# A hybrid retention and SSD layer on eight cores: convolution in one PSUM bank, the skip term on GpSimd, one matmul to spread four heads, and dependences kept by 8 bytes

## The reference

```python
h = x + hybrid_mixer(rmsnorm(x), w_in, ...)        # retention, 4 heads of 256; SSD, 16 heads of 64
y = rmsnorm(h + squared_relu_mlp(rmsnorm(h), w_up, w_down))
# in the mixer, for the SSD heads:
xbc = silu(causal_depthwise_conv(xbc, conv_w) + conv_b)     # 4 taps over time, 1536 channels
xs, bm, cm = split(xbc, [1024, 1280])
L = exp(where(causal, a_cs[l] - a_cs[s], -inf))             # per chunk of 128 tokens and head
y_diag = ((cm @ bm.T) * L) @ (xs * dt)
state  = exp(a_cs[-1]) * state + bm.T @ (xs * dt * exp(a_cs[-1] - a_cs))
y_ssd  = y_diag + exp(a_cs) * (cm @ state_before) + d_skip * xs
y_ssd  = rmsnorm_per_group(y_ssd * silu(z))
```

## Time and profile before

| | |
|---|---|
| median of 3 runs | 1701.88 us (1701.72 to 1702.16) |
| the profiled execution | 1701.95 us |
| its span, first to last instruction, slowest core (2) | 1700.4 us |
| spans of the eight cores | 1697.8 to 1700.4 us |
| mean granted TensorE clock, every core | 0.998 |
| PE busy | 1651.5 us, 97% |
| VectorE (DVE) busy | 704.2 us, 41% |
| ScalarE (ACT) busy | 404.0 us, 24% |
| GpSimd (POOL) busy, nearly all of it DMA issues | 66.3 us, 4% |

### The profile page before, as it was taken

The page is one execution under the profiler, slowest core; times in us unless marked ns, Lnnn a source line. Parts: engine busy times, 40 slices in busy tenths (PEclk is TensorE's granted clock), DMA queues, the critical chain, the costliest instruction groups (busy, mean ns, idle before and its releaser), DMA issues.

```text
span 1700.4 us, 26583 instructions; the slowest of 8 cores (1697.8 to 1700.4 us)
## 1 busy us (share of the span) xinstructions
PE 1651.5 (97%) x10277; PEld 962.3 (57%) x10410; DVE 704.2 (41%) x1300; ACT 404.0 (24%) x767; POOL 66.3 (4%) x127
## 2 busy tenths in 40 slices
PE   3999999999999999999999999999999999999997
PEld 2898888776666676545444444444444444444443
DVE  4577657777765555537312111212111211221235
ACT  4532325767622222102111001110001100011013
POOL 2000000000000000000000000000000000000000
PEclk9999999999999999999999999999999999999999
DMA  9965527333293264761854456443554443554425
GB/s 241 234 115 105 89 32 112 54 73 50 31 194 55 46 100 62 178 109 16 135 78 70 69 81 95 78 76 50 92 82 75 75 75 60 90 85 79 86 65 156
DMA packets 23099, 155.09 MB, mean 91 GB/s; under 512 B 2560, under 2 KB 2816, under 8 KB 5696
## 3 DMA queue, kind: packets, MB, share of 16 engines
q0 software_dynamic: 17648, 124.92, 45.1%
q1 hardware_dynamic: 5328, 28.48, 5.3%
HBM read 261.06 MB, written 8.39 MB: 158 GB/s over the span
## 4 chain that ended last, share of the span: by engine, by line
PE 94%; DMA 2%; DVE 1%; issue 1%; ACT 1%; DVEq 0%; POOL 0%; ACTq 0%; POOLq 0%
PE psum L513 92%; PE psum L516 2%; DMA arena<-xp 1%; DMA arena<-cstb 1%; DVE arena L541 1%; ACT arena L534 1%; DVE arena L550 0%; DVE arena L545 0%; ACT L534 0%; DVEq L372 0%; DVEq L391 0%; POOL arena L503 0%; ACTq L391 0%; POOLq L391 0%; POOLq L443 0%
## 5 line engine op out<-in xcount | busy, mean ns | idle before, releaser
L513 PE MATMUL psum<-arena 128*128 128x512 bf16 (+6 forms) x9541 | 1617.5, 329 | 13.8 <-DVE arena L541 4.9
L513 PEld LDWEIGHTS psum<-arena 128*128 128x128 bf16 x9674 | 917.0, 98 | 694.6 <-issue 12.8
L541 DVE TENSOR_TENSOR arena<-arena 128x512 bf16<-128x512 f32 (+6 forms) x351 | 191.1, 550 | 376.7 <-ACT arena L534 367.2
L534 ACT ACTIVATE arena<-psum 128x512 f32<-128x512 f32 (+4 forms) x234 | 130.9, 565 | 793.4 <-PE psum L513 759.2
L541 DVE TENSOR_TENSOR arena<-arena,psum 128x512 f32<-128x512 f32 x190 | 130.1, 687 | 367.7 <-PE psum L513 356.2
L534 ACT ACTIVATE arena<-arena 128x512 bf16<-128x512 f32 (+3 forms) x207 | 151.5, 744 | 377.2 <-DVE arena L541 174.5
L541 DVE TENSOR_TENSOR arena<-psum,arena 128x512 f32<-128x512 f32 (+5 forms) x250 | 175.6, 731 | 134.0 <-PE psum L513 111.8
L550 DVE SCALAR_TENSOR_TENSOR arena<-psum,arena 128x512 f32<-128x512 f32 (+1 forms) x164 | 112.0, 695 | 44.5 <-ACT arena L534 38.3
L534 ACT ACTIVATE arena<-psum,arena 128x128 f32<-128x128 f32 (+3 forms) x212 | 91.4, 514 | 108.8 <-PE psum L513 86.1
L516 PE MATMUL psum<-arena 128*128 128x128 bf16 x736 | 56.7, 225 | 24.9 <-DVE arena L545 24.7
L516 PEld LDWEIGHTS psum<-arena 128*128 128x128 bf16 x736 | 48.7, 101 | 32.8 <-issue 26.5
(11 more groups left out here) (18 smaller groups left out, 21.5 us busy)
## 6 DMA issues: line engine op xcount, KB each, us to landing
arena<-w_up POOLq DMA_DIRECT2D x32, 1024.0 KB, 10.9
arena<-w_down POOLq DMA_DIRECT2D x32, 1024.0 KB, 10.3
arena<-w_ret POOLq DMA_DIRECT2D x22, 1024.0 KB, 10.6
arena<-xm SPq DMA_DIRECT2D x16, 1024.0 KB, 10.4
arena<-w_xs POOLq DMA_DIRECT2D x8, 1024.0 KB, 10.9
arena<-w_out POOLq DMA_DIRECT2D x8, 1024.0 KB, 10.9
arena<-xp POOLq DMA_DIRECT2D x7, 1024.0 KB, 26.9
y<-arena SPq DMA_DIRECT2D x14, 512.0 KB, 3.6
```

The costliest lines, as they stand in the source:

```text
L513: P.op("pe", lambda e: e.matmul(R(out), lhsT=lhsT, rhs=rhs, start=start, stop=stop), [lhsT, rhs], [out], c, lat=163.0)
L534: P.op("act", lambda e: e.activation(out=R(out), in_=R(in_), func=func, **kw), ins, outs, c, lat=0.0, table=table)
L541: P.op(eng, lambda e: e.tensor_tensor(out=R(out), in0=R(a), in1=R(b), op=op), [a, b], [out], dcost(out, True), lat=0.0)
```

## The change

- `XW` is 1024: no halo in `xnP` and `xnM`. `convtile` makes 512 columns at once in one bank, 16 matmuls (the first-block tiles of group 0 in P in two halves of 256). The taps that fall ahead of the tile come from `tail`: the last three PSUM columns of the tile before are copied, five small POOL operations combine them with the taps, and a 3-column addition puts them into the next tile. `chead` makes the last four columns of P for the two channel tiles that P doesn't compute.
- The skip term is a product on POOL of the transposed x with d_skip, added to `t1` on POOL; `dgh`, `dgl` and their matmuls go. The product for the state input and the decay of the state also move from DVE to POOL.
- `spread` holds the running sums of each of four heads in its own 128 columns, zero on the other heads' partitions (made with the mask `hm`), and 16 more rows with a mask by blocks of 8 tokens. One matmul of 512 columns then takes the place of the mask matmul and the four of a head. Inside a block of 8 the values above the diagonal can become large; the product with the decay takes the minimum with 1e30 first, and the scores are masked by `tri` as before.
- `GR` is 8. The planner's model gets other DMA figures, POOL is no longer held to the order of the text, operations on PSUM tiles that aren't on PE get a priority of 1000 places, and costs of small matmuls and of POOL change.
- The selection matrix is smaller and is loaded ahead of `dtM`; the transfer of the old mask goes.

```diff
-XW = 1028
+XW = 1024
-GR = 32
+GR = 8
-DMA_SHARE = {"sp": 1.0, "pool": 1.4}
-DMA_START = {"sp": 1500.0, "pool": 4000.0}
+DMA_PULL = {"sp": 0.5, "pool": 1.0}
+DMA_START = {"sp": 1500.0, "pool": 6000.0}
+AHEAD = 1000
-    INORD = ("pool", "sp")
+    INORD = ("sp",)
...
+        rank = list(range(len(recs)))
+        for ops in self.vops:
+            for i in ops:
+                if recs[i]["eng"] != "pe":
+                    rank[i] = i - AHEAD
...
+    def dcost(out, two, eng="dve"):
         n = float(np.prod(out.shape[1:]))
+        if eng == "pool":
+            return 200.0 + 2.2 * n
         return 150.0 + (1.045 if two else 0.55) * n
...
-    def convtile(xn, w, co, ch, blk, out):
-        p2 = bank("C", 2).rearrange("p (s n) -> p s n", s=2)
-        for s in range(2):
-            t0 = (2 * blk + s) * 256
+    tails = {}
+
+    def tail(ch, h):
+        k = tails.get(ch, 0)
+        tails[ch] = k + 1
+        cp(raw[:, ch, k % 2, :], h)
+        h, g, t = raw[:, ch, k % 2, :], head[:, ch, :], htmp[:, ch, :]
+        ts(g, h, cw[:, 0, ch:ch + 1], None, ALU.mult, eng="pool")
+        for j in (1, 2):
+            ts(t[:, 0:3 - j], h[:, j:3], cw[:, j, ch:ch + 1], None, ALU.mult, eng="pool")
+            tt(g[:, 0:3 - j], g[:, 0:3 - j], t[:, 0:3 - j], ALU.add, "pool")
+
+    def convtile(xn, w, co, ch, blk, out, parts=1):
+        p = bank("C")
+        n = 512 // parts
+        for s in range(parts):
+            t0 = blk * 512 + s * n
             for dc in range(16):
-                mm(p2[:, s, 0:260], w[:, dc, co:co + 128], xn[:, dc, t0:t0 + 260], dc == 0, dc == 15)
-        acc = accr().rearrange("p (s n) -> p s n", s=2)
-        act(acc, p2[:, :, 4:260], AF.Identity, scale=cw[:, 3, ch:ch + 1], bias=cb[:, ch:ch + 1])
+                mm(p[:, s * n:(s + 1) * n], w[:, dc, co:co + 128], xn[:, dc, t0:t0 + n], dc == 0, dc == 15)
+        acc = accr()
+        act(acc, p, AF.Identity, scale=cw[:, 3, ch:ch + 1], bias=cb[:, ch:ch + 1])
         for j in (2, 1, 0):
-            stt(acc, p2[:, :, 1 + j:257 + j], cw[:, j, ch:ch + 1], acc, ALU.mult, ALU.add)
-        act(out, acc.rearrange("p s n -> p (s n)"), AF.Silu, table="silu")
+            stt(acc[:, 3 - j:512], p[:, 0:509 + j], cw[:, j, ch:ch + 1], acc[:, 3 - j:512], ALU.mult, ALU.add)
+        if ch in tails:
+            tt(acc[:, 0:3], acc[:, 0:3], head[:, ch, :], ALU.add)
+        if xn is xnP or blk == 0:
+            tail(ch, p[:, 509:512])
+        act(out, acc, AF.Silu, table="silu")
+
+    def chead(w, co, ch):
+        p = bank("B")
+        for dc in range(16):
+            mm(p[:, 0:4], w[:, dc, co:co + 128], xnP[:, dc, 1020:1024], dc == 0, dc == 15)
+        tail(ch, p[:, 1:4])
...
-                mm(p, identb, negm, True, False)
-                for hh in range(4):
-                    h = g * 8 + q * 4 + hh
-                    mm(p[:, hh * 128:(hh + 1) * 128], SEL[0:96, h, :], asp[0:96, c * 128:(c + 1) * 128], False, hh == 3)
+                mm(p, SEL[:, g * 2 + q, :], spread[:, c].rearrange("p j t -> p (j t)"), True, True)
...
-            tt(M, Ls[c], cbs.unsqueeze(1).to_broadcast([128, 8, 128]), ALU.mult)
+            stt(M, Ls[c], 1e30, cbs.unsqueeze(1).to_broadcast([128, 8, 128]), ALU.min, ALU.mult)
...
+            tt(v3(xD), v3(xt[:, 0:512]), dskc[:, g * 8:(g + 1) * 8].unsqueeze(2).to_broadcast([128, 8, 64]), ALU.mult, "pool")
             tt(v3(t1), v3(pYo), bh(EA, c, g), ALU.mult)
+            tt(t1, t1, xD, ALU.add, "pool")
             pYd = bank("B")
             for t in range(4):
-                cs = slice(t * 128, (t + 1) * 128)
-                mm(pYd[:, cs], xsT[par][:, t, tsl], dgh[:, g * 4 + t, :], True, False)
-                mm(pYd[:, cs], xsT[par][:, t, tsl], dgl[:, g * 4 + t, :], False, False)
                 for hh in (2 * t, 2 * t + 1):
-                    mm(pYd[:, hh * 64:(hh + 1) * 64], M[:, hh, :], xt[:, hh * 64:(hh + 1) * 64], False, hh == 2 * t + 1)
+                    mm(pYd[:, hh * 64:(hh + 1) * 64], M[:, hh, :], xt[:, hh * 64:(hh + 1) * 64], True, True)
             tt(t1, t1, pYd, ALU.add)
             if c < 7:
-                tt(v3(xcd), v3(xt[:, 0:512]), bh(DTDS, c, g), ALU.mult)
+                tt(v3(xcd), v3(xt[:, 0:512]), bh(DTDS, c, g), ALU.mult, "pool")
...
-                tt(v3(Sg), v3(Sg), bh(CD, c, g), ALU.mult)
+                tt(v3(Sg), v3(Sg), bh(CD, c, g), ALU.mult, "pool")
...
-    dma("pool", SEL.rearrange("p h n -> p (h n)"), cstb[:, B_SEL:B_END])
-    for k in range(8):
-        ts(dgh[:, k, :], ident, dskc[:, k:k + 1], None, ALU.mult)
-        stt(dgl[:, k, :], ident, dskc[:, k:k + 1], dgh[:, k, :], ALU.mult, ALU.subtract)
+    dma("pool", spread[96:128].rearrange("p c j t -> p (c j t)"), cstb[96:128, B_ROW:B_SEL])
+    a3 = asp.rearrange("p (c t) -> p c t", c=8)
+    for j in range(4):
+        ts(spread[0:96, :, j, :], a3[0:96], hm[0:96, j:j + 1], None, ALU.mult)
```

More of the change, by code:

```diff
@@ L212, in event @@
             live = [k for k in q if q[k] and q[k][0][2] <= now]
-            rate = {k: DMA_RATE * DMA_SHARE[k] / sum(DMA_SHARE[x] for x in live) for k in live}
+            rate = {k: DMA_RATE * q[k][0][3] / sum(q[x][0][3] for x in live) for k in live}
             times = [now + q[k][0][0] / rate[k] for k in live]
@@ L253, in advance @@
                         live = [k for k in dq if dq[k] and dq[k][0][2] <= dnow[0]]
+                        total = sum(dq[x][0][3] for x in live)
                         for k in live:
-                            dq[k][0][0] -= DMA_RATE * DMA_SHARE[k] / sum(DMA_SHARE[x] for x in live) * (limit - dnow[0])
+                            dq[k][0][0] -= DMA_RATE * dq[k][0][3] / total * (limit - dnow[0])
                     dnow[0] = max(dnow[0], limit) if limit < 1e17 else dnow[0]
@@ L534, in act @@
         P.op("act", lambda e: e.activation(out=R(out), in_=R(in_), func=func, **kw), ins, outs, c, lat=0.0, table=table)
-    def dcost(out, two):
+    def dcost(out, two, eng="dve"):
         n = float(np.prod(out.shape[1:]))
+        if eng == "pool":
+            return 200.0 + 2.2 * n
         return 150.0 + (1.045 if two else 0.55) * n
     def tt(out, a, b, op, eng="dve"):
-        P.op(eng, lambda e: e.tensor_tensor(out=R(out), in0=R(a), in1=R(b), op=op), [a, b], [out], dcost(out, True), lat=0.0)
+        P.op(eng, lambda e: e.tensor_tensor(out=R(out), in0=R(a), in1=R(b), op=op), [a, b], [out], dcost(out, True, eng), lat=0.0)
     def ts(out, a, s1, s2, op0, op1=ALU.bypass, eng="dve"):
@@ L565, in build_program @@
     CST = alloc([C_END], F32)
-    CB = alloc([B_SEL], BF16)
+    identb = alloc([128], BF16)
     SS = alloc([24, 8], F32)
-    NWT = alloc([32, 8], F32)
+    NWT = alloc([32, 2], F32)
     v0m = alloc([8, 256], BF16)
     pos_s = off[0]
-    SEL = alloc([16, 128], BF16)
+    spread = alloc([8, 4, 128], BF16)
     kv2 = at(pos_s, [2, 8, 256], BF16)
-    dgh = alloc([8, 128], BF16)
-    dgl = alloc([8, 128], BF16)
+    SEL = alloc([4, 128], BF16)
     SM = alloc([8, 8, 16], F32)
-    asp = alloc([1024], BF16)
+    xD = alloc([512], F32)
+    raw = alloc([12, 2, 3], F32)
+    head = alloc([12, 3], F32)
+    htmp = alloc([12, 3], F32)
     Sst = alloc([2, 512], F32)
@@ L957, in build_program @@
     mid = alloc([1024], BF16)
+    spot(pos_x + 8192)
+    asp = alloc([1024], BF16)
     spot(pos_t)
@@ L969, in dtM @@
             cp(acrep[:, :, 32 * r:32 * r + 16], SM[:, ACX])
-        pT = bank("C", 2)
-        for c in range(8):
-            mm(pT[0:96, c * 128:(c + 1) * 128], acrep[:, c, :], tri, True, True)
-        cp(asp[0:96, :], pT[0:96, :])
-        tt(r1[0:96, :], pT[0:96, :], asp[0:96, :], ALU.subtract)
+        for hf in range(2):
+            pT = bank("C")
+            for c in range(4):
+                mm(pT[0:96, c * 128:(c + 1) * 128], acrep[:, hf * 4 + c, :], tri, True, True)
+            a = slice(hf * 512, (hf + 1) * 512)
+            cp(asp[0:96, a], pT[0:96, :])
+            tt(r1[0:96, a], pT[0:96, :], asp[0:96, a], ALU.subtract)
         cp(mid[0:96, :], r1[0:96, :])
@@ L1005, in go @@
             def go(name=name, t=t, ch=ch, dst=dst):
+                if t == 5 and blk == 0:
+                    chead(W(name), 128, ch)
                 convtile(xnM, W(name), (t % 2) * 128, ch, blk, dst)
```

50 lines of the change are left out of this document (23 added, 27 removed).

## The result

The changed kernel takes 1692.65 us, the middle of two executions (1692.59 and 1692.72), against 1701.9 before. The ratio is 0.9945, 95% interval 0.9927 to 0.9962: 9.2 us less. The forecast was 1681 with a range from 1673 to 1692, so the time lies just outside it. Executions in which one die ran at a lower clock are left out here and in all that follows.

What follows compares the result with a forecast made beforehand. PE was taken as the bound, busy 1651.5 of 1700.4 us, with holes mainly before 62 us. 1701.9 - 16.5 (PE work) - 6 (start) + 2 (new holes) = 1681 us, range 1673 to 1692.

Steps and rivals of the forecast that it cites:

- PE's price list: PE matmuls, start to start: 215.75 ns for 512 columns, 110.6 for 260, 108.9 for 256, 57 for 128.
- The skip term: SSD stage on PE: 128 matmuls of 128 columns against the diagonals go, saving 7.3 us (7.1 to 7.8).
- the spread: Decay matrices on PE: 128 matmuls of 96 x 128 go, one of 512 columns per tile stays; saves 7.3 us.
- The convolution's 3.7 us: Convolution tiles on PE, mostly 512 columns at once: 155.7 us become 152.0; net 1.9 after 1.8 for the heads.
- The start: Before 62 us: unshared cells let chunk 0's readers start without chunk 7; gain 6 us, bounds -1 and +10.
- Rival (a): The start gives nothing, as the DMA and the written order decide: 1687 us; chance 0.15.
- 2 us of new holes: SSD stage: charge for denser PE and one more engine in the loop, bounds 6 more or 3 fewer.
- can't bind: SSD stage: only DVE operations with all operands in SBUF should collide with POOL; 40 more hidden us don't matter.
- Rival (c): SSD stage: POOL and DVE exclude each other in SBUF, 126 + 80 = 206 us against PE's 176: 1711; chance 0.07.
- twice DVE: SSD stage: a POOL operation of 512 columns was taken as 1.3 us, against DVE's 0.687 us.
- Rival (b): SSD stage latency bound: ACT and chains through POOL leave PE 6 to 12 us more holes, 1687 to 1693; chance 0.11.
- Rival (d): Weights come late behind computing in POOL's in-order queue, 20 us over some 10 issues: 1700 to 1703; chance 0.03.

Runs made afterwards that it cites:

- ad_load: `all_dve` plus 8 products of 256 columns on POOL, which nothing waits for, in each chunk step: 1694.55 us, ratio 0.9956.
- all_dve: The changed kernel with its four POOL operations of 512 columns (skip product, its addition, state-input product, state decay) on DVE: 1682.18 us, ratio 0.9884.
- halves0: `all_dve` with all ten convolution tiles of group 0 in P made in halves, not only the five first-block ones: 1681.47 us, ratio 0.9880.
- h0_cost105: `halves0` with the planner's fixed cost of a DVE operation at 105 ns for 150: 1686.49 us, ratio 0.9906.
- ad_inord: `all_dve` with POOL held to the order of the text again (`INORD = ("pool", "sp")`): 1693.95 us, ratio 0.9952.

## Why the prediction was wrong

**What bounds the kernel** was right: PE, everywhere but at the start; and most differences in this study follow from PE's work, its waits and its clock (in `ad_load` 9.7 of 12.4 us).

**PE's price list** was right as far as it was measured. The skip term was priced at 7.3 us and measured at 7.2; the spread was priced at 7.3 and its whole effect was 7.5, with the reserve made above. The heads' 32 matmuls of 4 columns, charged 1.8 us, are busy for 1.1 in all. The convolution's 3.7 us were not measured by themselves, but the sum closes: the profiled execution before, 1701.95, less 16.5, less 6 for the start, plus 3.0 for PE's waits in the stage (5.7 in `all_dve`, 2.7 before) makes 1682.4, and `all_dve` takes 1682.18. It closes with the forecast's own 6 us for the start, though, so an error there and one in the convolution could cancel.

**The start**, 6 us: right in its mechanism and about right in size. The aligned rows alone can't be told from the rest, but PE was busy for 39.29 us by 62.4 us, for 33.56 before, 5.7 more. The same cure in the old kernel, by 8-byte cells, gives 41.20 and 7.9 us in the end. Rival (a) is excluded.

**The failed step** is the charge of "2 us of new holes" for the SSD stage, and behind it the statement that the stretched DVE operations "can't bind". The stage got 10.4 us of waits (13.1 for 2.7) and, which no term foresaw, a lower granted clock in two windows of 20 us, 0.91 each, 3.6 us; `all_dve` has 1.00 in all of them. Put in place of the 2 us, they make 1701.9 - 16.5 - 6 + 10.4 + 3.6 = 1693.4, for 1692.65 measured. Of the 10.4 us, 3.0 are there in `all_dve` as well and so don't need POOL; from `all_dve` to the changed kernel it is 7.4 + 3.6 = 11.0 us, for a difference of 10.5. Rival (c) had the mechanism, DVE and POOL colliding in SBUF, and its partial form, and sized it by the sum of busy times: 126 us of DVE with some more below 176 of PE. That was the wrong test. DVE was busy 142 of 192 us in the bad kernel and 163 in the good one. What counts is not whether DVE has time on the average but whether a result comes when the written order wants it, and a product that takes 2.19 us for 1.22 in the middle of a chain can come too late by its whole stretch. The estimate "twice DVE" for a POOL operation was right. Two of the signs named beforehand failed: DVE's same forms were to "keep 0.687" and took 0.791, and PE's idle time in the SSD stage passed the 10 us that were to mean "wrong", with 13.2. Two others held: the first projection before 24 us (17.88), and POOL's operations at 1.12 to 1.39 us.

Rival (b), 1687 to 1693 with 6 to 12 us more of holes, gave the right time and the right holes (10.4), in part for another reason. It blamed ACT and the latency of the chains through POOL. ACT didn't become tighter: it was busy 124 of the 192 us, for 133 before, and in `all_dve` 132 with most of the holes gone. The chains through POOL may have a share (see below). Rival (d), late weights, is excluded: PE waited for a weight only once, 0.8 us at 17 us.

**Not settled.** How the 10.5 us divide between stretch, the delay of the chains over POOL and the written order. The delay is there. In the changed kernel DVE itself waits for POOL's results in this stage (total us, times, longest):

```profile
DVE arena L549 <- POOL arena L549: 8.3, 7, 2.9
```

In `all_dve` it doesn't. How much of these 8.3 us PE feels, no run tells. The loads for which nobody waits cost 0.11 and 0.14 us per microsecond of POOL, the real operations 0.10 to 0.17, so the stretch can explain all of it; but the real ones have other written orders, and these alone have been worth 3.5 to 11.8 us.

## What to carry to other kernels

Moving elementwise work from VectorE to GpSimd isn't free because GpSimd is idle: while it reads SBUF, VectorE operations with two SBUF operands take longer (686 to 832 ns here), and in a kernel whose engines run in a fixed order a late result can be paid at once, however low the busy share. Look at the mean of the same form before and after, and test with a load for which nobody waits: the written order of the others stays the same, and the difference is the sharing alone. And when dependences are kept by cells, look at what the layout makes them share: four columns of halo made the first chunk wait for the last, and one constant was worth 7.9 us, almost as much as the whole change.

## What the hardware showed that was not expected

A DVE product of 1024 columns with two SBUF operands takes 1.22 us alone, 1.46 on the average beside the POOL operations of the changed kernel, and 2.19 in the meeting shown above, where POOL ran without a break; 512-column operations of which one operand is in PSUM stay at 0.68 to 0.69. POOL memsets, 79.9 us of them, do nothing to either.

Short waits can cost twice. After a wait of 1.46 us in the changed kernel the matmuls run at the lower clock level for a while; timeline of PE on the slowest core, 370 to 382 us:

```profile
369.72 3.71 PE L519 MATMUL psum<-arena 128*128 128x512 bf16 x29
374.88 5.30 PE L519 MATMUL psum<-arena 128*128 128x512 bf16 x16 [1.46 <-DVE arena L562]
380.02 0.44 PE L522 MATMUL psum<-arena 128*128 128x128 bf16 x5
```

16 matmuls of 512 columns take 5.14 us until the next group, where 3.45 is usual: 1.7 us more than the wait itself, with a granted clock of 0.91 in these 20 us. But the same wait, before the same 16 matmuls, in the same execution, took no such price on cores 1, 3 and 5: there the 16 take 3.45 us and these 20 us have a granted clock of 1.00. So neither the length of the hole nor the written order around it decides this; it differs from core to core. Waits of 1.28 and 1.24 us in `all_dve` (363.87 and 407.84 us) left the clock at 1.00 as well.

And four kernels that do nearly the same work in another order, `halves0`, `all_dve`, `h0_cost105` and `ad_inord`, took 1681.5, 1682.2, 1686.5 and 1694.0 us. A planner whose own costs come nearer to the measured ones isn't thereby a better planner.
